# TensorE runs passes of ones by ones in the opening of a two-block network kernel

## What is computed

```python
mod = jax.nn.silu(c) @ w_ada[layer] + b_ada[layer]
shift, scale, gate = jnp.split(mod[:, None, :], 3, axis=-1)
h = rms_norm(x, norm_g[layer]) * (1.0 + scale) + shift
proj = h @ w_in[layer]
(hq, hf, hi, hz, rq, rk, rv, rz, ga, gb) = jnp.split(proj, offsets, axis=-1)
```

## Time and profile before

| | |
|---|---|
| median of 3 runs | 1606.76 us |
| lowest and highest run | 1606.14 and 1606.98 us |
| the profiled execution | 1606.08 us |
| its span, first to last instruction | 1604.3 us |
| TensorE products busy | 1575.4 us, 98% |
| VectorE busy | 1034.2 us, 64% |
| ScalarE busy | 819.0 us, 51% |
| POOL busy | 827.6 us, 52% |

### The profile page before, as it was taken

The page is one execution under the profiler, slowest core; times in us unless marked ns, Lnnn a source line. Parts: engine busy times, 40 slices in busy tenths (PEclk is TensorE's granted clock), DMA queues, the critical chain, the costliest instruction groups (busy, mean ns, idle before and its releaser), DMA issues.

```text
span 1604.3 us, 26217 instructions
## 1 busy us (share of the span) xinstructions
PE 1575.4 (98%) x9821; PEld 1364.5 (85%) x9821; DVE 1034.2 (64%) x1643; ACT 819.0 (51%) x1335; POOL 827.6 (52%) x459
## 2 busy tenths in 40 slices
PE   6999999999999999999999999999999999999997
PEld 4888888888888778568998998988788998998995
DVE  6886586686676869977743753755666762572554
ACT  4555455354364645467642542554667652453452
POOL 2554354445345448827754664654215665564653
PEclk9999999999999999999999999999999999999999
DMA  9321322322322356803332232352111333233231
GB/s 376 137 104 67 118 92 78 117 81 77 119 78 78 135 102 161 204 27 106 106 118 79 105 112 85 105 180 96 55 52 66 106 105 105 92 105 118 79 118 66
DMA packets 52774, 172.89 MB, mean 108 GB/s; under 512 B 5307, under 2 KB 9948, under 8 KB 52188
## 3 DMA queue, kind: packets, MB, share of 16 engines
q1 hardware_dynamic: 46432, 159.97, 29.3%
q10 hardware_dynamic: 6268, 11.95, 3.2%
HBM read 165.54 MB, written 6.36 MB: 107 GB/s over the span
## 4 chain that ended last, share of the span: by engine, by line
PE 91%; DVE 3%; ACT 2%; issue 2%; POOL 1%; DMA 1%; DVEq 0%; SPq 0%; POOLq 0%; ACTq 0%
PE gps L1985 15%; PE gps L1987 15%; PE gps L1986 15%; PE gps L2393 6%; PE gps L2395 6%; PE gps L2394 6%; PE aps L2393 3%; PE aps L2395 3%; PE aps L2394 3%; PE gps L2043 2%; PE gps L2044 2%; PE gps L2045 2%; PE gps L2330 2%; PE aps L2152 1%; PE aps L2224 1%
## 5 line engine op out<-in xcount | busy, mean ns | idle before, releaser
L608 POOL TENSOR_TENSOR w_lo<-w_raw,w_hi 128x1024 fp32r<-128x1024 f32 x172 | 441.4, 2570 | 501.3 <-ACT w_hi L730 501.0
L1985 PE MATMUL gps<-xa_hi,w_hi 128*128 128x512 f32 x767 | 305.3, 398 | 1.6 <-DVE xa_lo L1363 1.6
L1987 PE MATMUL gps<-xa_hi,w_lo 128*128 128x512 f32 x767 | 299.5, 391 | 0.0
L1986 PE MATMUL gps<-xa_lo,w_hi 128*128 128x512 f32 x767 | 299.5, 390 | 0.0
L730 ACT CAST w_hi<-w_raw 128x1024 fp32r<-128x1024 f32 x172 | 179.9, 1046 | 157.9 <-PE gps L1987 75.3
L1985 PEld LDWEIGHTS gps<-xa_hi,w_hi 128*128 128x128 f32 x767 | 144.3, 188 | 35.2 <-issue 3.6
L1987 PEld LDWEIGHTS gps<-xa_hi,w_lo 128*128 128x128 f32 x767 | 144.3, 188 | 30.8
L1986 PEld LDWEIGHTS gps<-xa_lo,w_hi 128*128 128x128 f32 x767 | 144.5, 188 | 27.8
L1985 PE MATMUL gps<-xb_hi,w_hi 128*128 128x512 f32 x384 | 150.6, 392 | 0.0
L1987 PE MATMUL gps<-xb_hi,w_lo 128*128 128x512 f32 x384 | 149.5, 389 | 0.0
L1986 PE MATMUL gps<-xb_lo,w_hi 128*128 128x512 f32 x384 | 149.5, 389 | 0.0
(11 more groups left out here) (412 smaller groups left out, 4341.6 us busy)
## 6 DMA issues: line engine op xcount, KB each, us to landing
w_raw<-weights_dram SPq DMA_DIRECT2D x268, 512.0 KB, 3.4
ada_w<-ada_in_dram SPq DMA_DIRECT2D x8, 1024.0 KB, 18.0
gates<-ret_tab_dram ACTq DMA_DIRECT2D x4, 1024.0 KB, 6.4
spread<-glu_scratch_dram SPq DMA_DIRECT2D x12, 270.0 KB, 5.0
rel_scratch_dram<-rel_rows ACTq DMA_DIRECT2D x1, 3072.0 KB, 34.5
x<-x_turned_dram SPq DMA_DIRECT2D x2, 1024.0 KB, 7.4
res<-xT_dram ACTq DMA_DIRECT2D x1, 2048.0 KB, 8.3
bias<-rel_scratch_dram ACTq DMA_DIRECT2D x1, 2048.0 KB, 9.3
```

What stands on the lines that cost most here:

```text
L608: TT(w_lo[:, j, :], w_raw[:, j, :], w_hi[:, j, :].bitcast(F32), ALU.subtract).then_inc(lo_ready[j], 1)
L1985: mm(gps[:, j, :], w_hi[:, j, w], x[0][:, k, :], start=k == 0, stop=False)
L1986: mm(gps[:, j, :], w_hi[:, j, w], x[1][:, k, :], start=False, stop=False)
L1987: last = mm(gps[:, j, :], w_lo[:, j, w], x[0][:, k, :], start=False, stop=k == blocks - 1)
```

## The change

A helper issues a number of products of the ones by the ones, 128 columns each in float32r, into the first 128 columns of a bank that the opening uses later (each starts afresh, and the bank's first real product starts afresh as well, so nothing of them stays). Such passes are put ahead of the transposes (40), ahead of the sums of squares (24), between `shift_sums(0)` and `shift(0)` (4), behind `shift(0)` (8) and between `shift_sums(1)` and `shift(1)` (4). The first 40 wait for the ones alone. All 80 are in TensorE's queue only; no other queue and no semaphore changes.

```diff
             xa, xb = (xa_hi, xa_lo), (xb_hi, xb_lo)
             pe.wait_ge(made, 1)
+            def idle_passes(n):
+
+                for _ in range(n):
+                    mm(gps[:, 2, 0:P], ones_r[:], ones_r[:], start=True, stop=True)
+
+            idle_passes(40)
             pe.wait_ge(c_col_ready, 2)
             pe.wait_ge(ident_loaded, 16)
             for k in range(KC):
                 last = mm(c_wide[:, k * P:(k + 1) * P], c_cols[:, k, :], ident[:], start=True, stop=True)
             last.then_inc(c_wide_ready, 1)
+            idle_passes(24)
             pe.wait_ge(mix_added, KC - 2)
             mm(aps[:, 0, :], ones[:], lnv[:], start=True, stop=False)
...
             shift_sums(0)
+            idle_passes(4)
             shift(0)
+            idle_passes(8)
             shift_sums(1)
+            idle_passes(4)
             shift(1)
             opening(0, 0, 1)
```

## The result

| | before | after |
|---|---|---|
| median of 13 runs each | 1608.07 us | 1611.13 us |
| lowest and highest | 1606.14 to 1608.94 us | 1610.44 to 1611.69 us |
| ratio of after to before | | 1.0022, 95% interval 1.0014 to 1.0029 |
| the profiled execution, its span | 1606.08 us, 1604.3 us | 1611.69 us, 1609.9 us |

The forecast was 1604.1 us with a range to 1606.9 us. The kernel became 3.1 us slower. The further runs of the kernel before also showed that its three first ones had been low: its runs stand in two groups, one near 1606.5 us and one near 1608.3 us. The traced execution of before (1606.08 us) is of the lower group, 2.0 us under its median, and the traced one of the changed kernel 0.6 us above its own; so the two traces lie further apart than the 3.1 us of the medians.

The account below looks back on a forecast made before the run. The opening's chain of waits, with TensorE at low clock until about 25.8 us, was taken as the bound. Gains 1.80 + 0.32 + 0.54 = 2.66 us off the 1606.76 us median gave 1604.1 us, range 1602.9 to 1606.9 us.

Parts of the forecast that it names:

- What the opening gains comes off the whole: Time the chain of waits gains before TensorE's last opening group at 45.79 us comes off the whole time.
- Price of a pass: Load of the ones plus float32r product of 128 columns on TensorE: 0.06 us at full clock, 0.107 us at low.
- 40 passes: cost nothing: Ahead of the transposes: 4.3 us from 2.38 us, ending at 6.7 us, 0.9 us before the identity at 7.63 us.
- The clock ahead of the sums: TensorE nearly unbroken from 2.4 to 13.9 us, so its clock has risen before the sums and holds over 2 us pauses.
- Rival 1: Passes as dear as float32 (0.47, then 0.235 us): sums end at 23.4 us, whole 1612.7 us; chance 6%.
- rival 2: Passes don't raise the clock ahead of the sums, which run 1.1 us later at the old speed: 1607.9 us; chance 8%.
- The sums themselves: Two products of sums on TensorE, 12.86 to 16.66 us: 2.00 us at full clock instead of 3.80, gain 1.80 us.
- First shift, gain 0.32 us: Shift's start at 18.40 us to ScalarE's reading: 0.63 us becomes 0.31, releasing POOL's step and VectorE's gain step earlier.
- Product at 24.64 us, gain 0.54 us: TensorE product in the opening: start to ScalarE's reading of the shift falls from 1.65 us to 1.11 us at full clock.
- rival 3: The wait passes to weight landings: the fifth pair holds the chain at 27.9 us, gain 1.7 us, 1605.1 us; chance 10%.
- rival 4: 160 more instructions shift TensorE's later code; loop repeats gain or lose waits, 2 to 5 us either way; chance 6%.
- a rise during the sums: If the unprofiled runs' clock already rose during the sums, the change's gain would be nearer 1.5 us.

Follow-up runs that it names:

- the two other traces with the 40 passes: The changed kernel cut to the 40 passes ahead of the transposes (1608.46 us), and the changed kernel with POOL's second low part waiting for VectorE's second input step (1608.7 us).
- wide version: Changed kernel with 10, 6, 1, 2 and 1 passes of 512 columns in place of 40, 24, 4, 8 and 4 of 128: 1607.0 us.
- wide version with POOL's wait: Passes of 512 columns in the changed kernel, and POOL's second low part waits for VectorE's second input step: 1606.26 us, ratio 0.9993 to the kernel before.
- dense version: Changed kernel with 512-column passes filling nearly all TensorE pauses, and POOL's second low part waiting for VectorE's second input step: 1604.38 us, ratio 0.9983 to the kernel before.
- the second and the third trace: The unchanged kernel before, profiled two more times: executions of 1606.47 us and 1606.9 us.
- without the collision: Changed kernel with all passes, but POOL's second low part waits until VectorE has ended its second input step: 1608.7 us.
- with the passes short enough not to stand in the way: Changed kernel with 20 and 8 narrow passes in place of 40 and 24, and POOL's second low part waiting for VectorE's second input step: 1605.23 us.
- the same wait: Kernel before, with only POOL's second low part made to wait until VectorE has ended its second input step: 1606.14 us, ratio 0.9992.

## Why the prediction was wrong, point by point

- **What the opening gains comes off the whole.** Right; the last column above shows it, for losses too.
- **Price of a pass: the first step that failed.** The term "40 passes: cost nothing" was mis-sized. I took 0.107 us and 0.06 us; it is 0.220 us and 0.110 us. The rows had both bounds, and I chose by type and columns. The float32r stream of 256 columns at 0.12 us allowed two readings, bound by its columns or by its loads, and I halved it by the first. The 40 passes ended at 11.2 us instead of 6.7 us, their cover of 0.9 us was gone, and the transposes started 3.40 us late.
- **The clock ahead of the sums.** I took it that the clock would rise with the passes. 8.8 us of them left it low, and it rose at 14.40 us, as the transposes ended; in the two other traces with the 40 passes it rose later still (15.61 and 15.39 us). So the price at the low clock held for all 40. Rival 1 had a price too high and a clock that rises after nine passes, rival 2 a clock that stays low and the cheap price. The truth was half of each. I had priced my two doubts one at a time; together they let the sums start 4.25 us late. By rival 1's own turning point, about 0.14 us a pass at the full clock, the measured 0.110 us alone would not have eaten the gain.
- **The sums themselves.** Right in size: 1.9 us at the full clock instead of 3.8 us, 2.0 forecast. But they ended at 19.0 us instead of 16.66 us, and VectorE's first input step came 2.40 us later (20.60 less 18.20).
- **First shift, gain 0.32 us.** Wrong in sign. From its start to ScalarE's reading it did fall, from 0.63 us to 0.42 us (20.80 to 21.22 us). But that moved POOL's step from 0.19 us behind VectorE's step to 0.02 us ahead of it, for 1.29 us net. I had read that POOL holds VectorE, in the gain step, and did not ask which step it would meet if POOL came earlier. The Trainium skill (SBUF — State Buffer, SBUF: two separate sides) says that of a VectorE operation with two SBUF inputs and one of GpSimd that reads SBUF, the one that starts first gets the shared ports for its whole length and the other fully blocks. The traces agree, with a margin of 0.02 us.
- **Product at 24.64 us, gain 0.54 us.** Not there: it ran at 28.33 us with 0.79 us. I took it that a risen clock stays through pauses of 2 us, from the end of the program, where TensorE stops after long dense work. Here it had been sparsely busy, the pause grew to 3.13 us, and the clock fell at 28.05 us, 0.28 us ahead of this product. In the wide version it fell with no pause over 1.84 us, and in the wide version with POOL's wait it held over one of 2.04 us: the length of one pause does not decide it in these traces.
- **The landing of the fifth pair (rival 3).** It came where the rest was put right: 0.90 us of wait in the dense version, whose gain at the last group against the first trace of before is 1.89 us and not 2.66.
- **Code (rival 4).** Nothing to see: the last column above moves by 0.3 us for up to 160 instructions more.
- **The base.** The forecast stood on one execution whose clock rose at 25.8 us. In the second and the third trace it was up before the sums, at 11.30 and 11.53 us. I named a case near to that (a rise during the sums, 1.5 us of gain left) and gave it no chance of its own. The base was low as well: of the 7.0 us between forecast and result 1.3 us are the median of before (1608.07 instead of 1606.76 us), 2.7 us the gain that did not come, and 3.1 us the loss.

The size, by differences of medians from the changed kernel downwards: 1611.13 us; without the collision 1608.7 us, 2.4 us less, a part of it clock; with the passes short enough not to stand in the way 1605.23 us, 3.5 us less. These two terms sum to 5.9 us and are the loss, with a gain of about 2.8 us against before below them. These are differences of whole kernels: how much of each term is the clock is not separated. The kernel before pays the collision itself in some runs, and with the same wait it comes down to 1606.14 us.

## What to carry to other kernels

Filler work costs its place in the queue at the clock that it finds, not at the one that it hopes to make; count it by a measured row of the same shape, and where none is there, put the dear end to the test before anything else. Before an engine is sped up, list which long operations will then start side by side: here 0.2 us decided whether POOL's 2.4 us stood in VectorE's way. And where the runs of a kernel stand in two groups, one trace is one of its cases, so take two or three before a stretch is costed to a tenth of a microsecond.

## What the runs showed of the hardware that was not expected

- A float32r product with its load costs 0.11 us at the full clock for 64, 128 and 192 columns alike and 0.12 us for 256, and 0.22 us at the low clock for 128.
- The clock can stay low through long unbroken work, and like work ends differently from one execution to the next. 8.8 us of passes of 128 columns left it low in three traces. With the same ten passes of 512 columns ahead it rose at 5.40, 7.06, 7.61 and 11.54 us. The same transposes of 3.75 us were followed by a rise at 11.30 us in the second trace of before, and in the first by sums that ran wholly at the low clock.
- In a sparsely used opening the clock can fall again after pauses of under 2 us, and can also hold over one of 2.04 us. In the two traces with the pauses filled by wide passes it held from 7.1 and 7.6 us to the end of the work.
- The granted clock in the profile reads full up to the first change on record, also where the durations say half.
